# Layer 1's modulation summed during layer 0's experts, its first norm a stage of its own, semaphores cleared by ranges

## The reference, cut to what matters

```python
for l in range(2):
    mod_l = silu(c) @ w_mod[l] + b_mod[l]          # (1, 6144)
    mod_c = silu(c_ctx) @ w_mod[l] + b_mod[l]      # the same for the context
    sh1, sc1, g1, sh2, sc2, g2 = split(mod_l, 6)   # csh1 .. cg2 from mod_c
    hl = rmsnorm(x, norm1_w[l]) * (1 + sc1) + sh1  # hc likewise, of ctx
    # three mixers (SSD, RWKV-7, neighbourhood attention) from h @ w_in[l], merged
    x = x + g1 * merged
    toks = rmsnorm(x, norm2_w[l]) * (1 + sc2) + sh2
    # 2 of 16 SwiGLU experts per token (hidden 768)
    x = x + g2 * moe(toks)
```

## Time and profile before

| | |
|---|---|
| median of 3 runs | 4389.47 us (4385.0 to 4389.6) |
| profiled execution | 4385.84 us, its span 4384.1 us |
| TensorE busy (matmuls) | 4005.9 us, 91% |
| VectorE, ScalarE, POOL busy | 1383.7, 1013.4, 455.3 us |
| DMA | 539.20 MB, mean 123 GB/s |
| granted TensorE clock, mean | 0.958 |

### The profile page before, as it was taken

How to read it: one execution, slowest core, us unless ns; L and a number is a source line. 1 busy time by engine, 2 the same in 40 slices (tenths; PEclk the granted TensorE clock), 3 DMA queues, 4 the chain that set the end, 5 groups by cost and what they waited for, 6 DMA issues and landing times. The chain is left out here.

```text
span 4384.1 us, 94494 instructions
## 1 busy us (share of the span) xinstructions
PE 4005.9 (91%) x42596; PEld 2712.0 (62%) x42596; DVE 1383.7 (32%) x2784; ACT 1013.4 (23%) x1735; POOL 455.3 (10%) x360
## 2 busy tenths in 40 slices
PE   5999998999999999879999588998999999998996
PEld 2454445448887785368878235656678887874332
DVE  1471004235555461110000145202255555512111
ACT  2121005124343331100000122103143443311101
POOL 0050002101111110000000002102011111100000
PEclk8999999999999999979999798999999999998998
DMA  7201222220000011349998631223201000146996
GB/s 306 77 1 58 86 62 64 96 57 19 19 19 19 21 42 40 140 166 315 324 309 285 247 136 39 87 77 106 79 19 35 19 19 21 42 138 255 404 403 269
DMA packets 299414, 539.20 MB, mean 123 GB/s; under 512 B 52320, under 2 KB 160112, under 8 KB 298880
## 3 DMA queue, kind: packets, MB, share of 16 engines
q1 hardware_dynamic: 291392, 505.80, 33.4%
q0 software_dynamic: 7616, 27.27, 1.7%
HBM read 515.13 MB, written 17.87 MB: 122 GB/s over the span
## 5 line engine op out<-in xcount | busy, mean ns | idle before, releaser
L1470 PE MATMUL bank<-inv 64*64 64x64 f32 x15104 | 487.9, 219 | 19.0 <-ACT inv L1793 8.5
L1470 PEld LDWEIGHTS bank<-inv 64*64 64x64 f32 x15104 | 467.4, 135 | 56.5 <-issue 54.7
L1014 PE MATMUL bank<-sb_h,sb_ring 128*128 128x512 f32 (+1 forms) x1344 | 480.4, 517 | 14.3 <-DMA sb_ring<-w_branch 7.0
L1014 PEld LDWEIGHTS bank<-sb_h,sb_ring 128*128 128x128 f32 x1344 | 257.8, 193 | 230.2 <-issue 198.3
L2665 PEld LDWEIGHTS bank<-xs,gu 128*128 128x128 f32 x3072 | 347.3, 193 | 8.6 <-issue 7.4
L2665 PE MATMUL bank<-xs,gu 128*128 128x96 f32 x3072 | 347.3, 276 | 1.0 <-DVE hid L2594 1.0
L1480 PE MATMUL bank<-sb_h,sb_ring 128*128 128x512 f32 (+1 forms) x672 | 276.8, 566 | 6.2 <-DMA sb_ring<-w_in 4.1
L264 PE MATMUL bank<-sb_h,sb_ring 128*128 128x512 f32 x512 | 224.7, 602 | 17.4 <-SPq L229 17.4
L1480 PEld LDWEIGHTS bank<-sb_h,sb_ring 128*128 128x128 f32 x672 | 128.7, 193 | 138.5 <-issue 129.3
L264 PEld LDWEIGHTS bank<-sb_h,sb_ring 128*128 128x128 f32 x512 | 98.8, 193 | 141.7 <-issue 124.2
L2490 PE MATMUL bank<-gu,xs 128*64 128x512 f32 x768 | 169.8, 594 | 9.0 <-DMA gu<-moe_w_up 8.5
(11 more groups left out here) (391 smaller groups left out, 5939.6 us busy)
## 6 DMA issues: line engine op xcount, KB each, us to landing
mod_ring<-w_mod SPq DMA_DIRECT2D x24, 2048.0 KB, 22.7
sb_ring<-w_in SPq DMA_DIRECT2D x24, 2048.0 KB, 7.8
gu<-moe_w_gate SPq DMA_DIRECT2D x128, 384.0 KB, 8.7
gu<-moe_w_up SPq DMA_DIRECT2D x128, 384.0 KB, 10.0
sb_ring<-moe_w_down SPq DMA_DIRECT2D x96, 512.0 KB, 4.5
gu<-moe_w_gate SPq DMA_DIRECT2D x64, 768.0 KB, 14.0
gu<-moe_w_up SPq DMA_DIRECT2D x64, 768.0 KB, 14.9
sb_ring<-moe_w_down SPq DMA_DIRECT2D x32, 1024.0 KB, 14.8
```

The source lines that it names most:

```text
L1014: mm = nc.tensor.matmul(out, left(kt), right(kt), start=kt == 0, stop=kt == KT - 1)
L1470: m = mm(bank[hs, at:at + w], left(hs), right(hs), start=start, stop=True, skip_group_check=True)
```

## The change

Layer 0's `experts_rows` sums layer 1's modulation beside its rounds (`ModAhead`): SP loads `w_mod[1]` in 48 tiles of 512 KB into `k.acc`, four places, four tiles in each of 12 groups; VectorE multiplies each by `silu(c)` per partition and adds, for both vectors, in `tok` once POOL has placed the rows; every eight tiles it transposes and reduces. TensorE adds the partitions up with a `selector` after round 12, VectorE finishes after `hid` of round 13. SP asks for the first slabs of layer 1's `w_in` after the last `down`, in `experts_rows`. Layer 1 starts with `norm_first` in place of `modulation`. `phase` clears runs of adjacent semaphore numbers by one instruction each. The diff, cut:

```diff
@@ -166,8 +166,12 @@
     _phase[0] += 1
     sems = namedtuple("Semaphores", names)(*(nc.alloc_semaphore(name=f"{n}_{_phase[0]}") for n in names.split()))
     yield sems
-    for s in sems:
-        nc.sync.sem_clear(s)
+    numbers = sorted(s.num for s in sems)
+    for i, a in enumerate(numbers):
+        if i == 0 or numbers[i - 1] + 1 < a:
+            first = a
+        if i + 1 == len(numbers) or a + 1 < numbers[i + 1]:
+            nc.sync.sem_clear(range(first, a + 1))
     for s in _cleared:
         nc.release_semaphore(s)
     _cleared[:] = sems
@@ -208,6 +212,10 @@
     wb = k.d.w_branch[k.layer, arg].rearrange("(kt p) c -> p kt c", p=P)
     at = C_GATE + D * arg + 256 * h
     return [(merge_slab(k, h)[:, 0], wv[:, :, at:at + 256]), (merge_slab(k, h)[:, 1], wb[:, :, 256 * h:256 * h + 256])]
+
+def slab_plans(d, l):
+    return [("plain", d.w_in[l], C_XBC), ("plain", d.w_in[l], C_Z), ("merge", d.w_in[l], 1), ("plain", d.w_out[l], 0)]
...
@@ -314,11 +322,8 @@
         @block.scalar
         def _(act):
             def squares(act):
-                if l == 0:
-                    act.wait_ge(s.tokens, 16)
+                act.wait_ge(s.tokens, 16)
                 for m in range(KT):
-                    if l:
-                        act.wait_ge(s.updated, m + 1)
                     if m >= 3:
                         act.wait_ge(s.summed, m - 2)
                     nc.scalar.activation(sq[:, m % 2] if m else k.ssq[:], k.x[:, m], ACT.Square).then_inc(s.square, 1)
@@ -381,12 +386,6 @@
         def _(v):
             nc.vector.memset(sc[:], 0.0).then_inc(s.padded, 1)
             do = Steps(v, s.vec)
-            if l:
-                for m in range(KT):
-                    for c in range(2):
-                        x = k.x[:, m, LC * c:LC * c + LC]
-                        ins = nc.vector.scalar_tensor_tensor(x, k.acc[:, m, LC * c:LC * c + LC], k.mod[:, 40 + m, c:c + 1], x, ALU.mult, ALU.add)
-                    ins.then_inc(s.updated, 1)
             for m in range(1, KT):
                 v.wait_ge(s.square, m + 1)
                 if m >= 2:
@@ -411,6 +410,106 @@
             v.wait_ge(s.affine, 2 * KT)
 
+
+def norm_first(k):
+
+    nc, l = k.nc, k.layer
+    with ExitStack() as st:
+        s = st.enter_context(phase(nc, "updated moved square summed root normed affine"))
+        sq = st.enter_context(nc.sbuf_tensor(f"sq_first{l}", [P, 3, TT], F32))
+        rinv = st.enter_context(nc.sbuf_tensor(f"rinv_first{l}", [P, TT], F32))
+        block = st.enter_context(nc.Block())
+        sums = k.bank[0]
+
+        @block.vector
+        def _(v):
+            for m in range(KT):
+                for c in range(2):
+                    x = k.x[:, m, LC * c:LC * c + LC]
+                    ins = nc.vector.scalar_tensor_tensor(x, k.acc[:, m, LC * c:LC * c + LC], k.mod[:, 40 + m, c:c + 1], x, ALU.mult, ALU.add)
+                ins.then_inc(s.updated, 1)
+            v.wait_ge(s.updated, KT)
+            nc.vector.tensor_copy(k.mod[:], k.next_mod[:]).then_inc(s.moved, 1)
+            v.wait_ge(s.root, 2)
+            for m in range(KT):
+                nc.vector.tensor_tensor(k.h[:, m], k.x[:, m], rinv[:], ALU.mult).then_inc(s.normed, 1)
+
...
+                nc.tensor.matmul(sums, const(k, "ones"), sq[:, m % 3], start=m == 0, stop=m == KT - 1).then_inc(s.summed, 1)
...
+        @block.scalar
...
+                nc.scalar.activation(sq[:, m % 3], k.x[:, m], ACT.Square).then_inc(s.square, 1)
+            act.wait_ge(s.summed, KT)
+            inverse_root(k, act, rinv[:], sums, s.root)
+            act.wait_ge(s.moved, 1)
+            for m in range(KT):
+                act.wait_ge(s.normed, m + 1)
+                for c in range(2):
+                    x = k.h[:, m, LC * c:LC * c + LC]
+                    nc.scalar.activation(x, x, ACT.Identity, bias=k.mod[:, m, c:c + 1], scale=k.nscale[:, 0, m, c:c + 1]).then_inc(s.affine, 1)
...
+class ModAhead:
+
+
+    TILES, RING, A_TURN = 48, 4, 4
+
...
+    def add(self, v, do, i, loaded, free):
+        nc, b, kt = self.k.nc, i // KT, i % KT
+        v.wait_ge(loaded[i % self.RING], 16 * (i // self.RING + 1))
+        tile = self.ring[:, i % self.RING]
+        for c in range(2):
+            by = self.silu[:, kt, c:c + 1]
+            if kt == 0:
+                do.put(nc.vector.tensor_scalar(self.acc[c], tile, by, None, ALU.mult))
+            else:
+                do.put(nc.vector.scalar_tensor_tensor(self.acc[c], tile, by, self.acc[c], ALU.mult, ALU.add))
+        do.settle()
+        v.sem_inc(free, 1)
+        if kt == KT - 1:
+            for c in range(2):
+                do.do(nc.vector.transpose(self.turned, self.acc[c]))
+                do.do(nc.vector.tensor_reduce(self.part[:, c, b], self.turned.rearrange("p (n q) -> p n q", q=32), AX.X, ALU.add))
+
+    def sums(self, bank):
+
+        nc = self.k.nc
+        for j in range(4):
+            parts = self.part.rearrange("p c b (m j) -> p j (c b m)", j=4)[:, j]
+            mm = nc.tensor.matmul(bank[32 * j:32 * j + 32, 0:96], self.selector, parts, start=True, stop=True)
+        return mm
+
+    def finish(self, do, bank):
+        k, nc = self.k, self.k.nc
+        mod, at, cols = k.next_mod, COLS["b_mod"][0], k.cols[:, self.layer]
+        for c in range(2):
+            do.do(nc.vector.tensor_tensor(mod[:, :, c], bank[:, 48 * c:48 * c + 48], cols[:, at:at + 48], ALU.add))
+        for n, (name, first) in enumerate((("norm1", 8), ("norm2", 32))):
+            for c in range(2):
+                w = cols[:, COLS[name][0]:COLS[name][0] + 8]
+                do.do(nc.vector.scalar_tensor_tensor(k.nscale[:, n, :, c], mod[:, first:first + 8, c], 1.0, w, ALU.add, ALU.mult))
 
 def norm_tokens(k, t0, *cleared):
@@ -2539,21 +2638,37 @@
     nc, l = k.nc, k.layer
     R, C, q = EXPERTS, SLOTS, k.pool_dma
     with ExitStack() as st:
-        s = st.enter_context(phase(nc, "turned xs_in silu hid ys_in weighed mixed back acc_in"))
+        s = st.enter_context(phase(nc, "turned xs_in silu hid ys_in weighed mixed back acc_in mod0 mod1 mod2 mod3 mod_free mod_vec mod_sum mod_done silu_c selector"))
 
         def sb(name, *shape):
             return st.enter_context(nc.sbuf_tensor(f"{name}{l}", [P, *shape], F32))
 
         row, xs, hid, ys = sb("xrow", 3, D), sb("xs", KT, C), sb("hid", 2, HT, C), sb("ys", 2, D)
+        silu, selector = sb("next_silu", KT, 2), sb("next_selector", 32)
         block = st.enter_context(nc.Block())
         wide, outs = k.bank[2:5], k.bank[5:7]
         row_in, stored, got = (q.row0, q.row1, q.row2), (q.stored0, q.stored1), (q.got0, q.got1, q.got2, q.got3)
         first = tok
+        ahead, mod_in = ModAhead(k, l + 1, k.acc[:].rearrange("p (a b) c -> p a (b c)", a=4), tok, silu, selector[:]), (s.mod0, s.mod1, s.mod2, s.mod3)
+        groups = ahead.TILES // ahead.A_TURN
         second = ws.gu[:].rearrange("p j e w c -> p (j e w c)")[:, 0:NT * D].rearrange("p (t c) -> p t c", t=NT)
 
         @block.sync
         def _(sp):
-            ws.rest_late(sp)
+            def ask_rows(g):
+                for i in range(ahead.A_TURN * g, ahead.A_TURN * g + ahead.A_TURN):
+                    ahead.ask(sp, i, mod_in, s.mod_free)
+
+            sp.dma_start(selector[:], k.d.selector).then_inc(s.selector, 16)
+            ask_rows(0)
+            for r in range(R):
+                ws.ask_gu_of(sp, r)
+                if 2 <= r <= groups:
+                    ask_rows(r - 1)
+                if r:
+                    ws.ask_down_of(sp, r - 1)
+            ws.ask_down_of(sp, R - 1)
+            ask_next_slabs(k, sp, [(ws.down_free, HT * R)] * 2)
 
         @block.gpsimd
         def _(pool):
@@ -2580,6 +2695,7 @@
             for i in range(2):
                 pool.wait_ge(stored[i], 16 * (R // 2))
             pool.wait_ge(ws.gu_free, R * KT)
+            pool.wait_ge(s.mod_done, 1)
             for t in range(NT):
                 for c, buf in enumerate((first, second)):
                     nc.gpsimd.indirect_dma_start(buf[:, t], None, k.d.rows_out, index(t, c), bounds_check=R * C - 1, oob_is_err=False)\
@@ -2587,11 +2703,24 @@
 
         @block.vector
         def _(v):
+            do = Steps(v, s.mod_vec)
             for r in range(R):
                 v.wait_ge(s.silu, r + 1)
                 h = hid[:, r % 2].rearrange("p f c -> p (f c)")
                 nc.vector.tensor_tensor(h[:, 0:2 * C], h[:, 0:2 * C], wide[1][:, 2 * C:4 * C], ALU.mult)
                 nc.vector.tensor_tensor(h[:, 2 * C:6 * C], h[:, 2 * C:6 * C], wide[2][:, 0:4 * C], ALU.mult).then_inc(s.hid, 1)
+                if r == 0:
+                    v.wait_ge(q.placed, 16 * 2 * NT)
+                    v.wait_ge(s.silu_c, 1)
+                if r < groups:
+                    for i in range(ahead.A_TURN * r, ahead.A_TURN * r + ahead.A_TURN):
+                        ahead.add(v, do, i, mod_in, s.mod_free)
+                if r == groups - 1:
+                    v.sem_inc(s.mod_sum, 1)
```

(21 more changed lines are left out.)

22 lines of the change are left out of this document (21 added, 1 removed).

## The result

The changed kernel took **4309.45 us** (median of 4 runs, 4306.75 to 4312.5) where the kernel before took 4388.43 on the same chip: a ratio of 0.9822, interval 0.9804 to 0.9839, 79 us less. Two repeats gave 4316.41 (0.9843, 0.983 to 0.9856) and 4313.8 us (0.9828, 0.9815 to 0.9842), 69 and 74 us less. 57 were forecast, and the range ended at 4316: the direction was right and the gain was set too small by 12 to 22 us. The profiled execution took 4310.02 us (span 4308.3; before 4385.84 and 4384.1).

What follows compares the result with a forecast made beforehand. TensorE, nearly full throughout, was taken to bound the kernel, so time could be won only where it dips. Terms -54.0 - 14 + 5 + 5 + 1 = -57 us led to 4331 us, range 4316 to 4357.

Steps and rivals of the forecast that it cites:

- Part 1: Between the layers: last expert copy to `conv_project`'s first product falls from 87.65 to 33.6 us, gain 54.0 (50.6 to 57.8).
- part 5: SP's clears between stages: as ranges 276 clears go, 15.7 us; gain taken as 14 us (0 to 15.7).
- Part 2: VectorE in layer 0's expert rounds: added work takes 15 to 24 us of a 32.4 us round, cost 0.
- Part 3: SP's queue and DMA in the expert rounds: 380 GB/s demanded fits 409, cost 0, upper bound 23 us.
- Rival B: Expert rounds run late: DMA capacity is 357 GB/s, 23 us late after 11 rounds; 4336 to 4354 us, chance 0.12.
- Rival D: Slower than before: `xrow` lands too late in the expert rounds; 4403 us if landing takes 25.2 us, chance 0.03.
- Part 4: Ends of layer 0's experts and modulation sums: start +5 us, end +5, sums +1.
- Rival C: End of layer 0's experts: gathers lose 5.3 us more to `w_in`, `conv_project` starts slow, +3.4; 4340 us, chance 0.10.
- Rival E: Start of layer 1: something still holds it for its modulation, such as `mod_done` late before the gathers; chance 0.01.
- rival A: Clears between stages: ranges cost as much as their single clears, +14 us, 4345 us; chance 0.12.
- The sum: Whole kernel: -54.0 - 14 + 5 + 5 + 1 = -57 us, giving 4331 us.

Runs made afterwards that it cites:

- single_clears: The changed kernel with its semaphores cleared one by one again: 4330.06 us, 0.9877 of the kernel before.
- late_close: The changed kernel with first `w_mod` tiles asked after the first rows' turn, `w_in` slabs after `rows_out` is stored: 4312.14 us, 0.9828 of the kernel before.
- warm_before: The kernel before, single clears kept, plus unread products on TensorE while it waits ahead of `branch_streams` (2) and `residual_out` (5): 4375.84 us, ratio 0.9981.
- ranges_only: The kernel before with only the change's `phase`, clearing each stage's semaphores as ranges: 4363.5 us, 0.9946 of the kernel before.

## Why the prediction was right and wrong

**Part 1, the stage between the layers: right, its size off by 3 us.** 54.0 forecast, 57.3 measured (87.65 - 30.3), inside the bounds. In single_clears, without the ranges, it is 31.2 us from the last copy to the first product, so 56.5 by the moved modulation itself. The sums ended 10.9 us after the first update (11.7 forecast), root and affine took 11.5 (11.4), as `norm_tokens` had shown. The first update came 0.8 earlier and the lead was 1.4 for 3.2; the part of it that went by the ranges, 0.8 us, had been counted in part 5 as well.

**Part 2, VectorE: right.** 11.9 and 15.6 us of 32 are within the room, and VectorE waits for its tiles, not TensorE for it. The transpose is 1.245 us and the reduction 1.220, for an estimate of 1.1.

**Part 3, SP's queue and the DMA engines: right.** The rounds hold 382 GB/s. The choice of 409 GB/s over the 357 worked out from the share was right as far as the 380 needed: 0.91 went with 315 GB/s and 1.02 with 383, so the share overstated the load at 315, and where the capacity ends was not reached. The reason given for it, that the share counts waiting, no run shows. Rival B falls. The Trainium skill (SBUF — State Buffer, Summary: rules for kernel authors) estimates transfers at about 358 GB/s; here one core alone took 382 for ten rounds, so the trace disagrees. Rival D falls too, `xrow` lands in 9.8 us. The Trainium skill (DMA: Bandwidth & Descriptors, queues, rings and completion order) has each engine go round robin between queues; that agrees with the 9.8 for 10.7 us in the rounds.

**Part 4, the ends and the sums: right, 9.6 for 11.** The start lost 4.6 us (8.62 - 4.03) for 5, the end 3.5 (7.1 for 3.6) for 5. Rival C, the gathers losing 5.3 more to the slabs, did not come: `rows_out` landed in 6.8 us and the gathers ran beside little. late_close shows that it was near: with the slabs asked 0.8 us ahead of the first gather, and not 9.0, a tile takes 4.1 for 2.5 us. The sums took about 0.7 us for 1. Rival E falls by the timeline.

**Part 5, the clears: here the forecast failed.** Its step was "If each becomes one range at the price of one clear, ... 276 go, 15.7 us". The waits bear that out (15.1 us), and rival A falls. The step priced a clear by SP's time alone and took the products behind it to cost what they cost before. Behind the idle time that SP's clears made, TensorE was at the 1.2 GHz level: at `branch_streams` of layer 0 the first seven instructions ran at 0.85 us rather than 0.43, at that of layer 1, with half the columns, at 0.43 rather than 0.22 (3.0 and 1.5 us in this pair of profiles); at `residual_out` it is 0.5 us in layer 0, where 2.1 us of idle time are left, and 1.5 in layer 1. The sum put this term at nothing; it is 6.5 us here, and warm_before, which takes all of it, measured 8.2 by itself. The part is worth 21 to 24 us, not 14. The rows for it were in hand: the earlier trace rows has the starts with 3.21 and 6.64 us of idle time, and part 1 used the same effect for `norm_first`.

**The sum.** With 21 to 24 us for the clears the forecast would have been 64 to 67 us, 4321 to 4324, still inside its range; the moved modulation had to bring more as well. single_clears gives it 54 for 43. Of these 11 the profiles place 4: 56.5 for 54 between the layers, 9.5 for 11 in the experts' stage. So 68 to 71 us are accounted for, against 69, 74 and 79 measured. The rest, up to 11, is not. In single_clears the stages of layer 1 behind its first one, whose code is that of the kernel before, are 9 us shorter in sum (1823.9 for 1832.8). TensorE's waits for `w_branch` in `branch_streams` and `rwkv_heads` have 2.7 of it (8.2 for 10.9 us; they are 9.8 to 11.3 in the four profiles without the moved modulation, ranges_only with 10.6 among them, and 8.2 to 8.7 in single_clears and the three of the changed kernel, so the drop goes with the moved modulation rather than with the clears), and why they fell is open. The rest of it may be scatter: from ranges_only to the three profiles of the changed kernel the same stages shrank by 8.0, 8.1 and 2.0 us.

## What to carry to other kernels

Work moved under a busy engine was free here up to a DMA share of 1.02, with each load asked about a round ahead; look for its price at the two ends of that stretch, where short transfers that someone waits for meet the long ones. When a wait ahead of TensorE is shortened, count the products behind it too: in this kernel an idle stretch of 3.2 us cost 3.0 us more behind it (1.7 in a second profile), and one of 1.1 us nothing. When a forecast has two parts, run each alone: here the sum hid that both were short. The profile's stages show whether an edit does what it should, the timed runs whether it lasts: the unused products here did the first and not the second.
